# Modulation row 1 of the first layer: six of sixteen units summed on VectorE, and ScalarE takes over the input copies and squares of the prologue

## The reference

```
silu_c = silu(c);  silu_cc = silu(c_ctx)
m_lat = split(silu_c @ ada_w[l] + ada_b[l], 9);  m_ctx = split(silu_cc @ ada_w[l] + ada_b[l], 9)

def rmsnorm(x, g):
    y = x * rsqrt(mean(x * x, axis=-1) + 1e-6)
    return y * g

def half_ffn(t, m, j):
    h = rmsnorm(t, norm_g[l, j]) * (1 + m[3*j+1]) + m[3*j]
    return t + 0.5 * m[3*j+2] * swiglu(h, w_gate, w_up, w_down)

x = half_ffn(x, m_lat, 0);  ctx = half_ffn(ctx, m_ctx, 0)    # l = 0: the first work of the program
```

## Time and profile before

| | us |
|---|---|
| median of three runs | 3337.91 |
| lowest and highest of the three | 3335.24, 3337.93 |
| the profiled execution | 3336.21 |
| its span | 3334.4 |
| TensorE busy | 3281.3 (98%) |
| VectorE busy | 2294.6 (69%) |
| ScalarE busy | 1274.4 (38%) |
| GpSimd busy | 648.4 (19%) |

### The profile page before, as it was taken

One profiled execution on the slowest core, in us unless ns is written; L12 is line 12 of the kernel. 1 busy time (PEld: TensorE's weight loads), 2 busy tenths in 40 slices (PEclk: granted clock), 3 DMA queues, 4 the chain that ended last, 5 costly groups with the idle time before them and its releaser, 6 DMA issues.

```text
span 3334.4 us, 49439 instructions
## 1 busy us (share of the span) xinstructions
PE 3281.3 (98%) x18955; PEld 2859.5 (86%) x18955; DVE 2294.6 (69%) x2888; ACT 1274.4 (38%) x1702; POOL 648.4 (19%) x535
## 2 busy tenths in 40 slices
PE   8999999999999999999999999999999999999999
PEld 4888888888888888887888889999888889999887
DVE  4878857878687636556776667856767676865766
ACT  3222233212321224334445344365534444456443
POOL 2202322212220230002242220000323240000222
PEclk9999999999999999999999999999999999999999
DMA  6655514646364433335665654445665655443664
GB/s 223 201 160 173 150 51 145 196 141 193 98 196 149 130 94 87 108 107 150 195 185 148 182 167 135 125 122 150 178 184 169 189 171 159 122 126 113 184 189 146
DMA packets 862984, 507.68 MB, mean 152 GB/s; under 512 B 15061, under 2 KB 843025, under 8 KB 862801
## 3 DMA queue, kind: packets, MB, share of 16 engines
q1 hardware_dynamic: 862432, 503.74, 51.6%
q0 software_dynamic: 368, 1.38, 0.1%
HBM read 504.01 MB, written 1.05 MB: 151 GB/s over the span
## 4 chain that ended last, share of the span: by engine, by line
PE 92%; DVE 4%; ACT 2%; issue 1%; SPq 0%; DMA 0%; POOL 0%; DVEq 0%; ACTq 0%
PE bank L613 18%; PE bank L611 18%; PE bank L615 18%; PE bank L614 18%; PE bank L609 10%; PE bank L608 2%; PE bank L1034 1%; DVE t_full L1562 1%; PE bank L722 1%; PE bank L885 1%; ACT whi_all L1111 1%; PE bank L754 1%; DVE wlo_all L1384 1%; PE bank L932 0%; PE bank L927 0%
## 5 line engine op out<-in xcount | busy, mean ns | idle before, releaser
L1384 DVE TENSOR_TENSOR wlo_all<-raw,whi_all 128x1024 fp32r<-128x1024 f32 (+3 forms) x768 | 1018.9, 1329 | 632.3 <-ACT whi_all L1111 629.5
L1111 ACT CAST whi_all<-raw 128x1024 fp32r<-128x1024 f32 (+3 forms) x768 | 833.5, 1089 | 866.6 <-PE bank L615 559.8
L613 PE MATMUL bank<-xn_two,whi_all 128*128 128x256 f32 (+1 forms) x2848 | 968.5, 340 | 6.0 <-DVE xn_two L1551 3.2
L614 PE MATMUL bank<-xn_two,whi_all 128*128 128x256 f32 (+1 forms) x2848 | 945.0, 332 | 0.0
L615 PE MATMUL bank<-xn_two,wlo_all 128*128 128x256 f32 (+1 forms) x2848 | 944.9, 332 | 0.0
L613 PEld LDWEIGHTS bank<-xn_two,whi_all 128*128 128x128 f32 x2848 | 540.4, 190 | 61.4 <-issue 6.6
L614 PEld LDWEIGHTS bank<-xn_two,whi_all 128*128 128x128 f32 x2848 | 540.6, 190 | 51.1 <-issue 0.7
L615 PEld LDWEIGHTS bank<-xn_two,wlo_all 128*128 128x128 f32 x2848 | 540.1, 190 | 51.6
L611 PE MATMUL bank<-xn_two,whi_all 128*128 128x512 f32 x1540 | 550.3, 396 | 0.0
L1978 POOL CAST h_two<-silu_g 128x256 f32 (+1 forms) x176 | 197.3, 1121 | 1378.8 <-DVE silu_g L1600 771.6
L609 PE MATMUL bank<-xn_two,wlo_all 128*128 128x256 f32 x1760 | 459.3, 281 | 3.2 <-DVE xn_two L1551 0.8
(11 more groups left out here) (281 smaller groups left out, 3835.2 us busy)
## 6 DMA issues: line engine op xcount, KB each, us to landing
raw<-in_ffn_w_in SPq DMA_DIRECT2D x176, 512.0 KB, 3.9
raw<-in_w_in SPq DMA_DIRECT2D x168, 512.0 KB, 3.9
ada_w<-in_ada_w SPq DMA_DIRECT2D x128, 512.0 KB, 4.1
raw<-in_ffn_w_gate SPq DMA_DIRECT2D x88, 512.0 KB, 3.8
raw<-in_ffn_w_up SPq DMA_DIRECT2D x88, 512.0 KB, 4.1
raw<-in_ffn_w_down SPq DMA_DIRECT2D x32, 768.0 KB, 5.3
raw<-in_ret_w_in SPq DMA_DIRECT2D x48, 512.0 KB, 3.9
raw<-in_ffn_w_out SPq DMA_DIRECT2D x32, 768.0 KB, 5.3
```

The lines of the kernel that those rows point to most:

```text
L613: pe.matmul(o, whi[s][:, k, :], hi, start=(k == 0), stop=False)
L614: pe.matmul(o, whi[s][:, k, :], lo, start=False, stop=False)
L1111: act.copy(whi[s][:, 0:ks, :], raw[s][:, 0:ks, :]).then_inc(hi_done[s], 1)
L1384: tt(wlo[s][:, 0:ks, :], raw[s][:, 0:ks, :], whi[s][:, 0:ks, :].bitcast(F32), ALU.subtract).then_inc(lo_done[s], 1)
```

## The change

Six of the eight units of row j = 1 no longer go through TensorE. VectorE multiplies each by the two silu scalars of its chunk and adds them up in `ada_acc[0]` and `ada_acc[1]` (12 instructions), and four matmuls (`first_rest`) with a selecting column, `first_sel`, add these sums over partitions into the same banks. The loading order becomes two units for TensorE and one for VectorE in turn; TensorE does four of its ten units ahead of the transposes, and the root sum stands behind all ten.

ScalarE takes over the eight copies of the transposed chunks and squares all chunks; GpSimd only adds, six instructions. The root is taken ahead of the casts. The fourth weight slot is split (cast and difference) behind the first chunk of the norm and no longer ahead of it.

```diff
-        first_order = [(j, k) for j in range(2) for k in range(DC)]
-        FIRST_AHEAD = 5
+        first_dve = [(1, k) for k in range(6)]
+        first_pe = [(0, k) for k in range(DC)] + [(1, k) for k in range(6, DC)]
+        first_order = [u for i in range(5) for u in (first_pe[2 * i], first_pe[2 * i + 1], first_dve[i])] + first_dve[5:]
+        FIRST_AHEAD, FIRST_PE_AHEAD = 5, 4
...
+            def first_rest():
+
+                pe.wait_ge(first_sel_ready, 1)
+                pe.wait_ge(first_sum, 2 * len(first_dve))
+                for half in range(2):
+                    for st in range(2):
+                        mm = pe.matmul(bank[half][0:4, :], first_sel[:, 1 - st:5 - st],
+                                       ada_acc[st][:, half * 512:(half + 1) * 512], start=False, stop=(st == 1))
+                    mm.then_inc(first_mm, 1)
...
-                for j, k in first_order[FIRST_AHEAD:]:
-                    if (j, k) == (1, 7):
-                        root_sum(a)
+                for j, k in first_pe[FIRST_PE_AHEAD:]:
                     first_unit(j, k)
+                root_sum(a)
+                first_rest()
                 root_spread(a)
...
             def do_first(a):
+                for k in range(DC):
+                    act.wait_ge(x_t, k + 1)
+                    act.copy(x[:, k, :], bank[4 + k % 4][:]).then_inc(x_in, 1)
+                    act.wait_ge(x_in, k + 1)
+                    if k == DC - 1:
+                        break
+                    if k >= 3:
+                        act.wait_ge(first_added, k - 2)
+                    act.activation(sumsq[:] if k == 0 else silu_g[(k - 1) % 2][:], x[:, k, :],
+                                   ACT.Square).then_inc(first_squared, 1)
+                act.wait_ge(first_added, DC - 3)
                 take_squares(a)
-                for s in range(SLOTS):
+                take_root(a)
+                for s in range(SLOTS - 1):
                     split_hi(s, 0, DC)
-                take_root(a)
...
+                    if a["n"] == 0 and k == 0:
+                        split_hi(SLOTS - 1, 0, DC)
...
-            for k in range(DC):
-                dve.wait_ge(x_t, k + 1)
-                dve.tensor_copy(x[:, k, :], bank[4 + k % 4][:]).then_inc(x_in, 1)
+            link(dve.memset(first_sel[:], 0.0))
+            link.after()
+            dve.memset(first_sel[:, 3:4], 1.0).then_inc(first_sel_ready, 1)
+            for n, (j, k) in enumerate(first_dve):
+                dve.wait_ge(first_landed[DC * j + k], 16)
+                for st in range(2):
+                    w, c, total = ada_first[DC * j + k][:], sil_c[:, k, st:st + 1], ada_acc[st][:]
+                    if n:
+                        dve.wait_ge(first_sum, 2 * n - 1 + st)
+                        stt(total, w, c, total, ALU.mult, ALU.add).then_inc(first_sum, 1)
+                    else:
+                        tsc(total, w, c, None, ALU.mult).then_inc(first_sum, 1)
...
             def do_first(a):
-                for s in range(SLOTS):
+                take_root(a)
+                for s in range(SLOTS - 1):
                     split_lo(s, 0, DC)
-                take_root(a)
...
+                    if a["n"] == 0 and k == 0:
+                        split_lo(SLOTS - 1, 0, DC)
                     if k and a["mode"] != "plain":
                         low(k - 1)
...
+                if a["n"] == 0:
+                    for k in range(1, DC - 1):
+                        pool.wait_ge(first_squared, k + 1)
+                        if k > 1:
+                            pool.wait_ge(first_added, k - 1)
+                        i = tt(sumsq[:], sumsq[:], silu_g[(k - 1) % 2][:], ALU.add)
+                        i.then_inc(first_added if k < DC - 2 else ss_done, 1)
+                    return
```

More of the change, by code:

```diff
@@ L322, in build @@
         ada_acc = [at(f"ada_acc{st}", [P, D], (110, 117)[st]) for st in range(2)]
+        first_sel = at("first_sel", [P, 7], 116)
         ada_group = at("ada_group", [P, 2, 32], 121)
@@ L416, in build @@
         first_cols = sem("first_cols")
+        first_sel_ready = sem("first_sel_ready")
+        first_sum = sem("first_sum")
+        first_squared = sem("first_squared")
+        first_added = sem("first_added")
         ada_landed = [sem(f"ada_landed{i}") for i in range(2)]
@@ L721, in first_unit @@
                 for half in range(2):
-                    mm = pe.matmul(bank[half][0:4, :], first_cs[:, j, k, :],
+                    pe.matmul(bank[half][0:4, :], first_cs[:, j, k, :],
                                    ada_first[DC * j + k][:, half * 512:(half + 1) * 512],
-                                   start=(j == 0 and k == 0), stop=(j == 1 and k == DC - 1))
-                    if j == 1 and k == DC - 1:
-                        mm.then_inc(first_mm, 1)
-            for j, k in first_order[:FIRST_AHEAD]:
+                                   start=((j, k) == first_pe[0]), stop=False)
+            def first_rest():
[6 more added lines that the diff above has]
+                    mm.then_inc(first_mm, 1)
+            for j, k in first_pe[:FIRST_PE_AHEAD]:
                 first_unit(j, k)
```

## The result

| | before | after |
|---|---|---|
| median, us | 3336.11 (20 runs) | 3340.99 (20 runs) |
| lowest, highest | 3334.71, 3338.82 | 3338.67, 3344.83 |
| profiled execution | 3336.21 | 3344.48 |
| its span | 3334.4 | 3342.7 |
| first matmul of the body starts at | 52.46 | 55.61 |

The ratio is 1.0013, with a 95% interval of 1.0007 to 1.0019: the changed kernel is slower by 4.9 us, clear of the scatter and still within 0.2%. Its profiled execution is the third longest of its 20, 3.5 us above their median, so its span is not to be set against the span before without care, and what its timeline shows need not have this size in every execution.

The account below looks back on a forecast made before the run. TensorE was taken to bound the kernel, so the body's first matmul decides: new matmuls' end -1.1, fourth split +2.9, second fall +1.6, sum +3.4 us; 3337.1 + 3.5 gave 3340.6 us, range 3335 to 3344.5.

Parts of the forecast that it names:

- Sums on VectorE: VectorE's prologue sums, taking turns with GpSimd's additions, end at 41.5 us (reckoned 41.4); 39.4 if turns cost nothing.
- TensorE's units and the root sum: Prologue on TensorE: transposes end near 27.1 us, last six units near 37.4, root sum at 39.3, deciding nothing.
- The new matmuls: Eight records on VectorE's sums: 3.4 us plus 1.5 for a clock fall, ending at 46.4 against 47.46.
- The moved split: Fourth difference, waiting for its cast, between first t_full and the body's first matmul: +2.9 us, bounds 1.2 to 3.2.
- The second fall: Low clock behind a gap of about 4.2 us ahead of the body's first matmul: +1.6 us, bounds 0 and 2.5.
- The sum: Whole kernel: new matmuls' end -1.1, fourth split +2.9, second fall +1.6, together +3.4 us.
- both clock terms: Clock falls at the new matmuls, +1.5 us, and at the first matmuls of the body, +1.6 us.
- the base: Time of the kernel before to which the forecast was added: 3337.1 us, middle of the four executions shown.
- The clock holds: Rival: one or both prologue clock falls stay out, or sums come at 39.4; -1.8 to +1.9 us; chance 0.27.
- The clock stays low throughout: Rival: clock low from the new matmuls to the end of the prologue, +7 to +8.6 us, 3344 to 3346; chance 0.09.
- The surplus is the whole story: Rival: TensorE's freed prologue time is all gained, 7 us faster, first matmul at 45.8; chance 0.02.
- The claim that the body is untouched: Behind the prologue nothing changes; a changed gap anywhere behind 60 us would refute it.

Follow-up runs that it names:

- the kernel that copies first: Kernel with five units on VectorE, ScalarE now copying four chunks of x before squaring any: 3335.81 us against 3336.64 for the kernel before, ratio 0.9998.
- both repairs: Changed kernel with the fourth split back ahead of the norm and nine filler matmuls ahead of the new matmuls: 3335.13 us against 3336.19, ratio 0.9996.
- the two that copy first: The kernel that copies first (3335.81 us), and the same with four filler matmuls ahead of the root sum (3333.68 us against 3336.35, ratio 0.9991).

## Why the prediction was right, and where it was off

It forecast 3340.6 us; 3340.99 was measured, and the way there held at nearly every step. Part of that closeness is luck.

- **Sums on VectorE.** Forecast to end at 41.4, measured 41.34. The step that carried it was the one that speaks against the change: the sum's instruction and GpSimd's addition take turns. The medians of 1.78 and 2.06 us show it, and with the additions left out the sums ended at 39.26 against the 39.4 given for free turns. The Trainium skill, SBUF — State Buffer, section "SBUF: two separate sides", states this lock; the trace agrees with it, 1.78 and 2.06 us against 1.27 and 1.26 alone. That the end fits to 0.1 us is luck: VectorE waited 1.35 us for a landing where 0.3 was allowed for waits, and its ten sums were busy for 17.2 us (2.48 and 14.70) where 18.2 were forecast.
- **TensorE's units and the root sum.** Transposes to 27.1 (26.94), units to 37.4 (37.3), root sum to 39.3 (39.2): right. That ScalarE's slower copies hold up the transposes was seen and rightly called harmless in this kernel; it was no longer harmless in the one with five units.
- **The new matmuls.** That the clock would fall behind the root sum was right, the size was off for this execution: 6.38 us, 4.9 were forecast. I let the low stretch be 3.4 us long and partly meet idle time. It took most of 7 us here (39.5 to 46.5 at a mean of 0.56), so the rows of mod came at 49.58 instead of 48.1, no sooner than before. With the split put back, behind the same gap, the records took 5.06, which is 1.5 over the 3.59 at full clock and just what the forecast had. So the term is 1.5 to 2.8; the execution that shows 2.8 is one of the slowest of its kernel, and which of the two is usual no run tells.
- **The moved split.** Forecast +2.9, measured +2.75 (5.34 against 2.59). Alone in the kernel before it showed +2.6 in the timeline.
- **The second fall.** Forecast +1.6, measured 2.4 (twelve matmuls at 0.43 instead of 0.23). The gap was 4.09 where 4.2 was forecast. Behind the same gap with the additions left out, some eight matmuls were slow, which is the 1.6 of the forecast. This term varies between executions too.
- **The sum.** The terms gave +3.4; in the profiled execution the head took +3.15 for the start and +2.4 for the slow matmuls, +5.6; the medians differ by 4.9. By this profile two errors met to put the forecast so near the measured time: both clock terms were too small, by 2.2 together, and the base was 1 us too high (3337.1 taken from four executions, 3336.11 by 20). Since the profiled execution is 3.5 us above the median of its kernel, the first of the two may be smaller in most executions.
- **The rivals.** *The clock holds* did not happen, but with filler it can be had: then the change costs 0.7 us. *The clock stays low throughout* did not happen: the high level was back from 46.5 to 53. For the low level at the start of the program, on which this rival leaned, the prediction had only the pace: the clock column reads 1.00 over 10 to 16 us of the kernel before. *The surplus is the whole story* fell as reckoned (the first matmul would have had to start at 45.5, not at 45.8 as written there, which changes nothing).
- The claim that the body is untouched holds for the work; it does not hold for the clock. The spans less the first matmul's start are 3281.9 before, 3287.1 after and 3283.5 with the split put back, of which 2.4 after lie in its first five us. Around 420 us both the kernel before and the one with the split put back have the root sum of a later norm, behind the same wait; that row of TensorE and the stretch from 419 to 424 us, first before, then with the split put back:

```profile
419.30 0.35 PE L754 MATMUL bank<-ones,sumsq 128*128 128x1 f32 x2 [0.42 <-ACT silu_g L1142]
...
419.00:424.00 5.00, 4.70 (x41) 4.68 (x42) 2.27 (x7) 2.14 (x5) 0.00 (x0) 1.00 0.37 107
```

```profile
418.35 0.35 PE L770 MATMUL bank<-ones,sumsq 128*128 128x1 f32 x2 [0.42 <-ACT silu_g L1169]
...
419.00:424.00 5.00, 5.00 (x32) 5.00 (x32) 0.77 (x5) 0.77 (x2) 0.00 (x0) 0.66 0.38 105
```

The same work met a low clock in the one and not in the other. The prediction had read two norms at which the clock fell, at 875 us behind 0.42 us and ahead of 505 us; at this one, in the same trace and behind the same 0.42, it held. Each kernel's median differs from what its first matmul and its slow matmuls make by up to 1.8 us (6.4 against 5.0 for the split alone; 0.85 against -0.9 for the split put back; 1.8 against 0 with the additions left out; -2.8 against -2.4 with five units). The profiles support that such low stretches in the body are the cause, without proving it. Read in stretches of 10 us from the first matmul on, the time at 1.2 GHz (twice what PEclk lacks of 1.00, summed) is 11.2 us in the shortest body (3281.1, five units), 15.0 in the kernel before (3281.9), 20.5 with the split put back (3283.5), and 26.2 and 23.9 in the two longest (3285.9 with the split alone, 3287.1 in the changed kernel). It is no strict rule: the kernel with filler in both gaps has 19.6 and a body of 3282.0. One profile stands for each kernel, and nothing here moves a fall in the body by itself; why a fall comes in one kernel and not in the other stays open.

## What to carry to other kernels

Work that moves off the bounding engine is won only if the engine that takes it is ready when it is asked: count what else that engine, and the engine that it takes turns with, has to do in the same stretch. Give the last arriving data to the engine that would otherwise wait for them; five units instead of six, together with the split behind the first full result, turned a loss of 4.9 us into a gain of 2.8 at the edge of what the medians can tell. A step that is moved behind the first chunk of a pipeline costs its length and that of the hand-over, here 1.22 us for the difference and 1.52 of waiting for its cast; behind the first full result, two steps on, it cost nothing that the timeline shows. A gap that can't be closed can be filled with matmuls that nobody reads: 24 of them won 4.1 us.

## What the runs showed of the hardware

A gap in TensorE's work costs more than its length. Gaps of 4.09 us were followed by matmuls at half pace in all three kernels that had one: twelve of them in the changed kernel and in the one with the split alone, some eight, from the fifth on, in the one without additions. A gap of 2.27 behind 1.9 us of one-column matmuls did the same, and 2.25 with the split put back. What I had not expected is how little can be enough: in the kernel that copies first, 0.68 us without work ahead of the root sum, as against none in the one with five units, went with 1.5 us more at the next matmuls. Their stretches from 40 to 44 us, first that with five units, then that which copies first:

```profile
40.00:44.00 4.00, 4.00 (x20) 2.00 (x21) 1.35 (x3) 2.40 (x4) 0.00 (x0) 1.00 0.73 182
```

```profile
40.00:44.00 4.00, 4.00 (x8) 0.93 (x8) 2.47 (x4) 3.30 (x5) 0.00 (x0) 0.57 0.59 142
```

The two stretches do not hold the same work, so their counts are not to be compared; what tells is the clock, 1.00 and 0.57, and the eight new records, 3.60 us in the first and 5.09 in the second. But the fall is no certainty behind such a wait. The root sum near 420 us stands behind 0.42 us without work in all eleven kernels, and in the one profiled execution of each the clock fell behind it in four (the split put back, both repairs, and the two that copy first) and held in seven, the kernel before and the changed one among them. So a short wait brings the fall in some executions and not in others, and a single profile can't tell how often.

On this the Trainium skill (TensorE: Matmul & The Clock Gate, section "Part 1: The HAM clock gate (the "warmup" mystery)") speaks of an idle array as what brings the low level. These rows add that the low level also followed short waits next to one-column matmuls, 0.42 and 0.68 us, some of the time, and that with filler in the gaps it did not come: no fall in the first 64 us of the changed kernel with filler, and none at the new matmuls of the two others that had it there.
